# The 32 columns of the value share move from a tile of their own into the rotary key's tile

## What is computed

```python
def forward(x):                                   # 2 layers, x: (1, 256, 1024) float32
    for i in range(2):
        x = x + 0.5 * swiglu(rms_norm(x), ffn1)   # D_FF 2816
        h = rms_norm(x)
        p_rw, p_cv, p_mla, p_gate = split(h @ w_in[i])      # 1920 | 1024 | 672 | 3072 columns
        y_rw, v_first = rwkv7_branch(p_rw, h, v_first, ...)
        y_cv = conformer_conv_branch(p_cv, ...)             # 31 taps
        y_mla = mla_branch(p_mla, cos, sin, ...)            # 8 heads
        x = x + sum(sigmoid(p_gate)_b * y_b) @ w_o[i]
        x = x + 0.5 * swiglu(rms_norm(x), ffn2)
# inside rwkv7_branch
    p = centred_shift_mix(p, mu)
    nu = jax.nn.sigmoid(v0 + (h @ v_down) @ v_up)           # v_down: 1024 x 32; not mixed
    v = v + (v_first - v) * nu                              # second layer only
# inside mla_branch
    cq, ckv, k_rope = jnp.split(p, [384, 640], axis=-1)     # k_rope: 32 columns, one for all heads
    k = concatenate([k_nope, broadcast(k_rope)])            # then rms norm and rotation by position
```

## Time and profile before

| | |
|---|---|
| median of three runs | 1732.7 us (1731.34 to 1738.39) |
| profiled execution | 1740.1 us, span 1738.1 us |
| mean granted TensorE clock | 0.964 of full speed |
| TensorE busy | 93% of the span |
| vector engine, scalar engine busy | 69%, 45% |
| stream loads | 417 of 512 KB, median 3.4 us to landing |
| chain that ended last | TensorE 79%, vector engine 8%, issue 6%, ACT 4%, DMA 3% |

### The profile page before, as it was taken

One profiled execution on the slowest core, in us unless ns is written; L12 is line 12 of the kernel. 1 busy time (PEld: TensorE's weight loads), 2 busy tenths in 40 slices (PEclk: granted clock), 3 DMA queues, 4 the chain that ended last, 5 costly groups with the idle time before them and its releaser, 6 DMA issues.

```text
span 1738.1 us, 43046 instructions
## 1 busy us (share of the span) xinstructions
PE 1608.8 (93%) x16861; PEld 1489.9 (86%) x16861; DVE 1203.0 (69%) x1784; ACT 778.3 (45%) x1195; POOL 94.7 (5%) x112
## 2 busy tenths in 40 slices
PE   6999999898978899999999999988999798999998
PEld 6999886778868789999889999867788686899997
DVE  4777675788675456777666786667887655667766
ACT  5444564472251245544444446534614412454444
POOL 1000020000020001000100002000000200010001
PEclk9999998999999999999999999989999898999999
DMA  5755531331021234555557555322311202445555
GB/s 184 270 183 183 182 122 61 98 100 61 27 74 39 87 102 161 190 182 181 191 182 243 182 185 175 103 74 85 110 39 39 82 21 85 144 151 195 182 183 193
DMA packets 62925, 231.55 MB, mean 133 GB/s; under 512 B 7024, under 2 KB 8048, under 8 KB 61840
## 3 DMA queue, kind: packets, MB, share of 16 engines
q1 hardware_dynamic: 61488, 221.41, 38.7%
q0 software_dynamic: 1248, 7.46, 1.2%
HBM read 228.09 MB, written 1.05 MB: 132 GB/s over the span
## 4 chain that ended last, share of the span: by engine, by line
PE 79%; DVE 8%; issue 6%; ACT 4%; DMA 3%; POOL 0%; DVEq 0%; ACTq 0%; SPq 0%; POOLq 0%
PE banks L545 16%; PE banks L546 15%; PE banks L547 15%; PE banks L612 9%; PE banks L613 5%; DMA raw<-in_stream 3%; PE banks L959 2%; PE banks L957 2%; DVE wlo L1443 2%; PE banks L948 1%; ACT whi L1108 1%; DVE arena L1882 1%; PE banks L837 1%; ACT arena L1286 1%; PE banks L723 1%
## 5 line engine op out<-in xcount | busy, mean ns | idle before, releaser
L1443 DVE TENSOR_TENSOR wlo<-raw,whi 128x1024 fp32r<-128x1024 f32 x417 | 511.5, 1230 | 302.0 <-ACT whi L1108 300.1
L1108 ACT CAST whi<-raw 128x1024 fp32r<-128x1024 f32 x417 | 436.3, 1050 | 456.4 <-PE banks L547 315.3
L545 PE MATMUL banks<-hx,whi 128*128 128x256 f32 x1696 | 489.6, 289 | 39.8 <-DVE wlo L1443 18.7
L546 PE MATMUL banks<-hx,whi 128*128 128x256 f32 x1696 | 485.1, 286 | 0.0
L547 PE MATMUL banks<-hx,wlo 128*128 128x256 f32 x1696 | 484.8, 286 | 0.0
L545 PEld LDWEIGHTS banks<-hx,whi 128*128 128x128 f32 x1696 | 330.6, 195 | 45.1 <-issue 32.3
L546 PEld LDWEIGHTS banks<-hx,whi 128*128 128x128 f32 x1696 | 330.8, 195 | 0.2
L547 PEld LDWEIGHTS banks<-hx,wlo 128*128 128x128 f32 x1696 | 330.7, 195 | 0.0
L545 PE MATMUL banks<-h,whi 128*128 128x256 f32 x896 | 272.4, 304 | 29.4 <-ACT arena L1206 17.6
L546 PE MATMUL banks<-h,whi 128*128 128x256 f32 x896 | 261.3, 292 | 0.0
L547 PE MATMUL banks<-h,wlo 128*128 128x256 f32 x896 | 260.4, 291 | 0.0
(11 more groups left out here) (291 smaller groups left out, 1869.3 us busy)
## 6 DMA issues: line engine op xcount, KB each, us to landing
raw<-in_stream SPq DMA_DIRECT2D x417, 512.0 KB, 3.4
arena<-in_wuq POOLq DMA_DIRECT2D x2, 1152.0 KB, 10.3
lo_w<-in_lora POOLq DMA_DIRECT2D x2, 1024.0 KB, 7.0
arena<-in_wukv POOLq DMA_DIRECT2D x2, 1024.0 KB, 13.5
xT<-in_x SPq DMA_DIRECT2D x1, 1024.0 KB, 5.0
out<-xT SPq DMA_DIRECT2D x8, 128.0 KB, 3.7
consts<-in_cst SPq DMA_DIRECT2D x1, 642.5 KB, 8.4
vec_t<-in_vecs POOLq DMA_DIRECT2D x3, 113.0 KB, 4.1
```

The source lines that it names most:

```text
L545: TE.matmul(o, wh, hi, start=first, stop=False, **kw)
L546: TE.matmul(o, wh, lo, start=False, stop=False, **kw)
L1108: SE.copy(whi[:, m % HL, :], raw[:, m % RAW, :]).then_inc(hi_ready, 1)
L1443: TT(wlo[:, m % HL, :], raw[:, m % RAW, :], whi[:, m % HL, :].bitcast(F), ALU.subtract)\
```

## The change

The tile `T_VD` goes. The last latent tile holds the rotary key's 32 columns once, in rows 0 to 31, and `v_down`'s 32 columns in rows 32 to 63; the rest is zero. The vector engine normalises each part by an instruction of its own. The weighted key has 32 rows, and the four copies arise on TensorE: four products with a 32 x 32 block of `rot` and four with one of the identity, each into another 32 rows of bank 3. The cosine's product therefore moves behind "k turned" and reads the bank. ACT's copy of the value share goes; its weights and products use rows 32 to 63. The filler plan of the pairs loses eight pieces: one from each "pair", one from each "mixed pair". Two taps move ahead of the first maximum. The number of tiles becomes 205.

```diff
--- before.py
+++ after.py
@@ -54,13 +54,12 @@
 LEVELS = 6
 
 
-N_RW, N_VD, N_MLA, N_CV = 15, 1, 6, 8
+N_RW, N_MLA, N_CV = 15, 6, 8
 T_FFN1 = 0
 T_MLA = T_FFN1 + 3 * NFF
 T_CV = T_MLA + N_MLA
 T_RW = T_CV + N_CV
-T_VD = T_RW + N_RW
-T_BR = T_VD + N_VD
+T_BR = T_RW + N_RW
 T_WO = T_BR + 3 * (RC + KC)
 T_FFN2 = T_WO + KC
 T_END = T_FFN2 + 3 * NFF
@@ -183,7 +182,7 @@
 PAIRS = RC
 FILL_A = {"latent squares": 12, "latents normed": 24, "squares": 20, "inverse": 10, "turned": 12, "scored": 20}
 for _p in range(PAIRS):
-    FILL_A.update({("pair", _p): 8, ("turned pair", _p): 6, ("mixed pair", _p): 9 + _p % 2})
+    FILL_A.update({("pair", _p): 7, ("turned pair", _p): 6, ("mixed pair", _p): 8 + _p % 2})
 FILL_R = {"key sums": 6, "decay": 8, "nu": 5, "values": 5}
 for _d in range(2):
     FILL_R.update({("kr", _d): (14, 16)[_d], ("tk", _d): (4, 6)[_d], ("pairs", _d, 0): (6, 20)[_d],
@@ -686,8 +685,8 @@
                             yield from tile_pieces(gates + e, bank[bank0 + (c + e) % nb][:, S:2 * S])
 
             def fill_r():
-                pe.wait_ge(*act.at(("column", T_VD - 1)))
-                pe.wait_ge(*act.at(("column", T_VD)))
+                pe.wait_ge(*act.at(("column", T_BR - 2)))
+                pe.wait_ge(*act.at(("column", T_BR - 1)))
                 pe.wait_ge(*vec.at(("u", 2, RC - 1)))
                 yield from branch_pieces(0, 2, 6, 2, u_hi, u_lo)
                 pe.wait_ge(*poo.at(("u", 1, RC - 1)))
@@ -726,7 +725,10 @@
                     m.then_inc(*ten.mark(("q", j // 2)))
             pe.wait_ge(*act.at(("k", 1)))
             pe.wait_ge(*vec.at("k rotary weighted"))
-            m = TE.matmul(bank[3][:, 0:S], cc("rot", P), krt, start=True, stop=True)
+            settled(pe)
+            for a, o in (("rot", 0), ("ident", S)):
+                for i in range(0, P, ROPE):
+                    m = TE.matmul(bank[3][i:i + ROPE, o:o + S], cc(a, ROPE, 0, ROPE), krt[0:ROPE, :], start=True, stop=True)
             m.then_inc(*ten.mark("k turned"))
             for t in range(NT):
                 for c in range(KVC):
@@ -875,9 +877,10 @@
                     lora(0, 1, (2, 3))
                     fr.at("decay")
                     pe.wait_ge(*act.at("key rms"))
+                    pe.wait_ge(*vec.at("value share in"))
                     for c in range(RC):
-                        m = TE.matmul(bank[4 + c // 2][:, (c % 2) * S:(c % 2 + 1) * S], lo_w[0:32, 3, c * P:(c + 1) * P],
-                                      wag[0:32, 3, :], start=True, stop=True)
+                        m = TE.matmul(bank[4 + c // 2][:, (c % 2) * S:(c % 2 + 1) * S], lo_w[ROPE:2 * ROPE, 3, c * P:(c + 1) * P],
+                                      wag[ROPE:2 * ROPE, 3, :], start=True, stop=True)
                     m.then_inc(*ten.mark("nu"))
                     fr.at("nu")
                     pe.wait_ge(*vec.at("key inverse"))
@@ -1199,14 +1202,11 @@
                                 sc.wait_ge(*vec.at(("glu", c - 2)))
                             SE.activation(gs[:, c % 2, :], bank[6 + c % 2][:, S:2 * S], ACT.Sigmoid)\
                                 .then_inc(*act.mark(("column", n)))
-                    elif n < T_VD:
+                    else:
                         i = n - T_RW
                         sc.wait_ge(*(vec.at(("mixed", i - 4) if i >= 4 else "pp edges")))
                         SE.copy(pp[:, i % 4, 1:S + 1], src[:, 0:S])
                         SE.mul(pt[:, i % 4, :], src[:, 0:S], mus[:, 0, i:i + 1]).then_inc(*act.mark(("column", n)))
-                    else:
-                        sc.wait_ge(*vec.at(("mixed", N_RW - 1)))
-                        SE.copy(wag[0:32, 3, :], src[0:32, 0:S]).then_inc(*act.mark(("column", n)))
                     hi(L, n + HL)
                     yield
 
@@ -1242,7 +1242,7 @@
             sc.wait_ge(*vec.at(("latent", QC + KVC - 1)))
             SE.activation(sq_lat, lat, ACT.Square).then_inc(*act.mark("latent squares"))
             sc.wait_ge(*vec.at(("latent", N_MLA - 1)))
-            SE.activation(kr_sq, rope_in, ACT.Square)
+            SE.activation(kr_sq[0:ROPE, :], rope_in[0:ROPE, :], ACT.Square)
             fa.at("latent squares")
             sc.wait_ge(*ten.at("latent norms"))
             SE.activation(nrm[:, 0, :], bank[0][:, 0:S], ACT.Sqrt, bias=cc("eps", 1, 0), scale=1.0 / QR)
@@ -1579,8 +1579,13 @@
 
             def latent(i):
                 used(T_MLA + i)
-                TT(lat[:, i, :] if i < QC + KVC else rope_in, bank[i][:, 0:S], rstd[:, 1, :], ALU.mult)\
+                rows = slice(0, P if i < QC + KVC else ROPE)
+                TT(lat[:, i, :] if i < QC + KVC else rope_in[rows, :], bank[i][rows, 0:S], rstd[rows, 1, :], ALU.mult)\
                     .then_inc(*vec.mark(("latent", i)))
+                if i == QC + KVC:
+                    rows = slice(ROPE, 2 * ROPE)
+                    TT(wag[rows, 3, :], bank[i][rows, 0:S], rstd[rows, 1, :], ALU.mult)\
+                        .then_inc(*vec.mark("value share in"))
 
             def h_rest(c):
                 ve.wait_ge(*act.at(("h hi", c)))
@@ -1616,7 +1621,7 @@
 
             def fill_a():
                 for n in range(T_CV, T_BR):
-                    if T_RW <= n < T_VD:
+                    if n >= T_RW:
                         shift_mix(n - T_RW)
                     lo(L, n + HL)
                     if n < T_RW and (n - T_CV) % 2:
@@ -1687,12 +1692,11 @@
             fa.at("latents normed")
             ve.wait_ge(*vec.at(("latent", N_MLA - 1)))
             ve.wait_ge(*act.at("latent squares"))
-            TS(krt, rope_in, vv("qk_k_r"), None, ALU.mult).then_inc(*vec.mark("k rotary weighted"))
-            ve.wait_ge(*vec.at("k rotary weighted"))
-            TT(kr0, krt, cosT[:, :], ALU.mult).then_inc(*vec.mark("k cosine part"))
+            TS(krt[0:ROPE, :], rope_in[0:ROPE, :], vv("qk_k_r", 0, 0, ROPE), None, ALU.mult)\
+                .then_inc(*vec.mark("k rotary weighted"))
             conv(16)
             ve.wait_ge(*ten.at("k turned"))
-            ve.wait_ge(*vec.at("k cosine part"))
+            TT(kr0, bank[3][:, S:2 * S], cosT[:, :], ALU.mult)
             TT(krt, bank[3][:, 0:S], sinT[:, :], ALU.mult).then_inc(*vec.mark("k sine part"))
             ve.wait_ge(*vec.at("k sine part"))
             TT(kr0, kr0, krt, ALU.add).then_inc(*vec.mark("k rotated"))
@@ -1745,7 +1749,7 @@
                 TT(u_lo[:, j, :], bank[4 + j % 2][:, 0:S], u_hi[:, j, :].bitcast(F), ALU.subtract)\
                     .then_inc(*vec.mark(("u", 2, j)))
 
-            conv(6)
+            conv(8)
             pair_max(0)
             pair_probs(0)
             fa.at("scored", 1)
@@ -2017,13 +2021,12 @@
         w_in = a["w_in"][l]
         for i in range(N_RW):
             T[T_RW + i] = col(w_in, i * P)
-        vd = np.zeros((D, P), f)
-        vd[:, :32] = a["rw_v_down"][r]
-        T[T_VD] = col(vd, 0)
         m0 = RW_COLS + CV_COLS
         for i in range(QC + KVC):
             T[T_MLA + i] = col(w_in, m0 + i * P)
-        T[T_MLA + QC + KVC] = col(np.tile(w_in[:, m0 + QR + KVR:m0 + MLA_COLS], (1, P // ROPE)), 0)
+        last = np.zeros((D, P), f)
+        last[:, :ROPE], last[:, ROPE:2 * ROPE] = w_in[:, m0 + QR + KVR:m0 + MLA_COLS], a["rw_v_down"][r]
+        T[T_MLA + QC + KVC] = col(last, 0)
         for c in range(RC):
             T[T_CV + 2 * c] = col(w_in, RW_COLS + c * P)
             T[T_CV + 2 * c + 1] = col(w_in, RW_COLS + CV + c * P)
@@ -2065,7 +2068,7 @@
         vecs[l, :, VEC["keep"]] = float(l > 0)
         vecs[l, :, VEC["first"]] = float(l == 0)
         lora[l, :, 2 * RW:3 * RW] = a["rw_g_up"][l]
-        lora[l, :32, 3 * RW:] = a["rw_v_up"][r]
+        lora[l, ROPE:2 * ROPE, 3 * RW:] = a["rw_v_up"][r]
         uq = a["mla_w_uq"][l].reshape(QC, P, H, QK)
         uq = np.concatenate([uq[..., :NOPE].reshape(QC, P, -1), uq[..., NOPE:].reshape(QC, P, -1)], 2)
         wuq[l] = uq.transpose(1, 0, 2).reshape(P, -1)
```

## The result

The changed kernel took **1754.6 us** in the median of four runs (1750.2 to 1759.6) beside 1732.0 for the kernel before (1730.2 to 1738.4): a ratio of **1.0128, interval 1.0097 to 1.0158**, some 22 us slower. The forecast was 1745.1 in 1735 to 1752. The sign was right, the size wasn't, and the time lies outside the range.

What follows compares the result with a forecast made beforehand. TensorE in the pairs was taken to wait for ACT's tile evacuations. Per layer +4.0 - 2.9 + 1.3 + 1.4 + 0.5 = 4.3, twice 8.6, plus 1.65 and 2.1: 12.4 us on 1732.7, 1745.1 us, range 1735 to 1752.

Steps and rivals of the forecast that it cites:

- What bounds the stage: Attention pairs: TensorE waits for ACT to evacuate filler tiles, so starting pieces count; idle 12.8 us against 8.75 per layer.
- 128: Piece position two pieces after turn 1 in the pairs: TensorE idle of 0.5 us.
- 88: Piece position inside "scored": TensorE idle grows from 1.10 to 1.9 us, behind two more vector taps.
- Removed work: Filler in the pairs: eight pieces fewer on TensorE, 2.9 us less per layer.
- the lora wait: Behind the pairs: lora products wait for tanh, after a later last R tile; 1.4 us more per layer.
- Rotation: Key rotation: one full product becomes eight small ones; 0.5 us more per layer, bounds 0.3 and 3.0.
- Layer change: Next layer's first tiles each move one place later in the ring, so TensorE restarts later: +1.65 us, once.
- End: Kernel's end: the last load's cast and remainder finish later, at 1740.2; +2.1 us, bounds 0 and 2.8.
- Clock: Pairs: granted clock falls behind the idle growing from 1.60 to 3.9 us; 1.3 us per layer, bounds 0 and 3.
- Rival 1: Pairs stay even: longer idle, no further clock loss, extra vector steps hidden, tanh delay absorbed; 1738 us, chance 20%.
- Rival 2: Removed products come off in full, since idle in the pairs only moves; 1729.6 us, chance 12%.
- Rival 3: Much slower: small key products don't overlap and the clock stays low for two pairs; 1754 us, chance 8%.

Runs made afterwards that it cites:

- Experiment 7: Kernel before with its filler plan moved on by eight pieces, all work kept; ratio 1.0045 to the kernel before.
- experiment 6: Changed kernel with the second empty tile moved from the layer's end to ahead of the branches: ratio 1.0071; with unread products ahead of the waits as well, 1.0013.
- Experiment 3: Changed kernel with 24 unread products per layer on TensorE, ahead of four waits in the pairs and the wait for tanh; ratio 1.0025 to the kernel before.
- experiments 9 and 10: Even piece plan, taps moved ahead of the pairs: changed kernel (second empty tile also moved) 1709.95 us, ratio 0.9858; kernel before 1714.8 us, 0.9871.
- 5: Kernel before with unread products on TensorE ahead of its own four waits of over a microsecond in the pairs; ratio 1.0004 to the kernel before.
- experiment 1: Changed kernel run again unaltered, beside the kernel before; ratio 1.0124.

## Why the prediction was wrong in size

- **What bounds the stage** (ACT's place behind the exponentials, not TensorE's work): right. All places of idle time came out, and all sizes within 0.2 us in two traces but for 128 (0.74 for 0.5) and the first, at 88, which was 1.71 to 2.63 for 1.9. Experiment 7 shows the cause apart: the shift of the plan alone, 8 us.
- **Removed work, 2.9 us per layer, and the lora wait, 1.4**: right in place; the wait measured 1.28. Idle, work and lora summed to +2.5 a layer; with all idle times filled in both kernels, so without a difference in clock, the stage is 108.3 against 106.3: +2.1.
- **Rotation** +0.57 for 0.5. The Trainium skill, "TensorEngine Tiling (Array Packing)", Key Properties, has a drain at a change of tiling; by the trace two changes and sixteen narrow instructions together take 1.00 us, so it is a small matter here.
- **Layer change** +1.77 for 1.65. **End**: +2.1 forecast, +1.6 in the first trace of after and +2.4 in the mean of thirteen traces (experiment 6). The chain of work still ends with that load (5.4 us before, 3.8 after), its cast and its remainder, as forecast. Right too.
- **Clock: the step that failed.** "A stretch like that of 1209, some 2.6 us at half speed, costs 1.3 us per layer (bounds 0 and 3)." I read one fall behind one idle, and too short (2.6 us, where the windows above have at least 3.2), missed the one behind 1.87 us, and gave one grown idle that price once. After has up to five such stretches a layer behind its idle times, about five microseconds each behind the two longest, and I priced none behind the lora wait, since its 1.3 us looked like a delay and nothing more. What the stage grew beyond the 2.1 is 7.8, 0.4, 6.1 and 6.0 us in the four layers traced, 5.1 in the mean, outside my bounds of 0 to 3. With 5.1 for 1.3 the sum would have been 12.4 + 7.6 = 20, and the median 1753; the interval of the measured 22 us is 17 to 27.
- **The range** was also drawn tighter than its own bounds. Its lower end, 1740, takes all the lower ones; all the upper ones (3.4 us of clock, 0.7 of the end, 5 of the rotation) give 1754 and not 1751.
- **Rival 1** (pairs stay even, 1738) took the clock at 1.00 behind the 1.60 us of the earlier trace rows as a sign that short idle times are free. Experiment 3, at 1740.3 us beside 1736.2, is about what that rival describes: it needs the idle times filled. Rival 2 needed the tile's work to count, which only the stages of experiments 9 and 10 show. Rival 3 had 2 us a layer more of low clock and 2.5 of rotation; the first came, at 3.8, the second didn't. That its 1754 is the measured time is luck: it had the rotation 5 us too dear.
- **The remainder**: the traces and the times divide the loss differently. The traces have some 10 us of clock (twice 5.1) and 4.1 (stages) + 1.1 (rotation) + 1.8 + 2.4 = 9.4 of the rest, beside 12.4 - 2.6 = 9.8 forecast. The times have 18 of clock and, by experiment 3 against 5, 0.21% of the rest, 3.6 us, -0.7 to 8. The granted clocks of all runs speak for the times. The traces are single executions: that of before is 7 us above its median and that of experiment 1 is 6 below its own, and stretches in which the kernels don't differ vary by 2 to 6 us between executions (the one behind the first key spread was 114.6, 114.2 and 110.0 us). How the 20 us divide is open between these two; that the clock is the term that was mis-sized isn't, since both have it far above 2.6.

## What to carry to other kernels

Where a stream of filler tiles is handed over through another engine's in-order queue, count at which piece each tile begins before removing or adding one; the phase was worth 8 us here, the tile perhaps 2 to 5 (not shown by time). Price a new idle time of a dense TensorE by more than its length: here the lost clock was 18 us by the times (11 to 24) and 10 by the traces, of 22 in all, and an experiment with unread products ahead of the wait, run in both kernels, separates the two. Then repair the phase rather than fill the waits: the even plan with the taps moved was 1.4% faster than the kernel before, the covers only came back to it.

## What the runs showed of the hardware

- The granted clock fell to 1.2 GHz behind twelve of the fifteen idle times of 1.87 to 3.75 us in the pairs of after and of experiment 1. The three without a fall were of 1.87, 3.04 and 2.63 us, so the length alone doesn't decide it. In before it fell behind 1.87 and 2.6 us and not behind 1.10 and 1.60. Nearly one list of idle times gave a mean of 0.84 in one layer and 0.92 in the next of the same execution; behind the same 3.75 us the first product after it was already slow (0.58 us) in layer 0, and in layer 1 two products went ahead at nearly full speed (0.38 and 0.31 us, then 0.40). So one trace gives a sample of this price and no value.
- An idle of 1.28 us stood ahead of sixteen products at 1.2 GHz in layer 0 (5.50 us) and at 2.4 GHz in layer 1 (3.72). Three unread products in its place made it 3.72 in both layers of experiments 3 and 4.
- Eight products of 32 rows by 32 columns over 256 columns, in two passes each, take 1.00 us. Their sixteen instructions start in fours, each four within 0.02 us and some 0.22 us behind the one before it, half of the 0.43 us that the two passes of the one full product take: those that write different rows of the bank overlap.
